# A fused two-block transformer kernel: relative bias skewed by DMA and spatial weights turned on VectorE, instead of on TensorE

## The reference, cut to what matters

```python
def diff_attention(q, k, v, lam, rel_bias):            # blocks of 128 queries
        bias = rel_bias[t5_bucket(kpos[None, :] - qpos[:, None])]   # (q, k, 4 heads)
        logits = jnp.where(mask, logits + bias[None, :, None], NEG_INF)
def gmlp_spatial_gate(u, vg, ln_g, ln_b, ws, bs):
    ws_m = jnp.where(mask[None], ws, jnp.zeros_like(ws))            # 8 groups of 128x128
    s = jnp.einsum('gij,bnjgc->bnigc', ws_m, vn) + ...
```

## Time and profile before

| what | value |
|---|---|
| median of 3 executions | 2445.34 us (2444.47 to 2445.42) |
| the profiled execution's own time | 2445.51 us |
| its span, first to last instruction | 2443.7 us |
| PE busy | 2425.7 us (99%) |
| DVE, ACT, POOL busy | 1378.2, 1161.1, 127.9 us |
| DMA queue of SP | 509.84 MB, 63.3% of 16 engines |
| mean granted TensorE clock | 0.998 |

### The profile page before, as it was taken

How to read it: one execution, slowest core, us unless ns; L and a number is a source line. 1 busy time by engine, 2 the same in 40 slices (tenths; PEclk the granted TensorE clock), 3 DMA queues, 4 the chain that set the end, 5 groups by cost and what they waited for, 6 DMA issues and landing times.

```text
span 2443.7 us, 28450 instructions
## 1 busy us (share of the span) xinstructions
PE 2425.7 (99%) x11416; PEld 2031.3 (83%) x11416; DVE 1378.2 (56%) x1113; ACT 1161.1 (48%) x1081; POOL 127.9 (5%) x144
## 2 busy tenths in 40 slices
PE   9999999999999999999999999999999999999998
PEld 7888888888888888888888889888888888888886
DVE  6877645656666666444555574554445444444445
ACT  5544554655556555333454364453343434433344
POOL 4000000001011110000000000000010100000000
PEclk9999999999999999999999999999999999999999
DMA  7566555587777777655565554556766767665553
GB/s 250 189 202 200 167 177 189 195 286 237 237 239 245 248 237 257 246 195 197 210 232 173 189 173 155 189 189 207 224 212 216 223 207 228 226 214 191 189 207 121
DMA packets 259456, 511.35 MB, mean 209 GB/s; under 512 B 10742, under 2 KB 33196, under 8 KB 258476
## 3 DMA queue, kind: packets, MB, share of 16 engines
q1 hardware_dynamic: 258936, 509.84, 63.3%
q10 hardware_dynamic: 436, 0.30, 0.0%
HBM read 482.83 MB, written 27.27 MB: 209 GB/s over the span
## 4 chain that ended last, share of the span: by engine, by line
PE 97%; ACT 1%; DVE 1%; issue 1%; DMA 0%; SPq 0%; DVEq 0%; ACTq 0%
PE ps L1256 28%; PE ps L1258 28%; PE ps L1257 28%; PE ps L1241 4%; PE ps L1242 2%; PE ps L1214 1%; PE ps L1250 1%; PE ps L1249 1%; PE ps L1248 1%; PE ps L1501 1%; ACT w_hi L683 1%; DMA raw<-in_w_in_dram 0%; DVE w_lo L1720 0%; PE ps L1516 0%; PE ps L1659 0%
## 5 line engine op out<-in xcount | busy, mean ns | idle before, releaser
L1720 DVE TENSOR_TENSOR w_lo<-raw,w_hi 128x2048 fp32r<-128x2048 f32 x427 | 988.1, 2314 | 1020.7 <-ACT w_hi L683 1020.4
L683 ACT ACTIVATE w_hi<-raw 128x2048 fp32r<-128x2048 f32 x427 | 818.5, 1917 | 1236.0 <-PE ps L1258 1113.7
L1256 PE MATMUL ps<-w_hi,xa 128*128 128x512 f32 x1856 | 724.8, 391 | 0.8 <-DVE w_lo L1720 0.8
L1258 PE MATMUL ps<-w_hi,xa 128*128 128x512 f32 x1856 | 723.0, 390 | 0.0
L1257 PE MATMUL ps<-w_lo,xa 128*128 128x512 f32 x1856 | 722.9, 390 | 0.0
L1256 PE MATMUL ps<-w_hi,g 128*128 128x512 f32 x1216 | 475.8, 391 | 0.0
L1258 PE MATMUL ps<-w_hi,g 128*128 128x512 f32 x1216 | 473.8, 390 | 0.0
L1257 PE MATMUL ps<-w_lo,g 128*128 128x512 f32 x1216 | 473.6, 390 | 0.0
L1256 PEld LDWEIGHTS ps<-w_hi,xa 128*128 128x128 f32 x1856 | 348.6, 188 | 73.9 <-issue 0.9
L1258 PEld LDWEIGHTS ps<-w_hi,xa 128*128 128x128 f32 x1856 | 348.5, 188 | 72.5
L1257 PEld LDWEIGHTS ps<-w_lo,xa 128*128 128x128 f32 x1856 | 348.6, 188 | 71.3
(11 more groups left out here) (316 smaller groups left out, 1367.8 us busy)
## 6 DMA issues: line engine op xcount, KB each, us to landing
raw<-in_ffn_w_dram SPq DMA_DIRECT2D x132, 1024.0 KB, 5.2
raw<-in_w_in_dram SPq DMA_DIRECT2D x95, 1024.0 KB, 5.2
raw<-in_w_up_dram SPq DMA_DIRECT2D x88, 1024.0 KB, 5.9
raw<-in_w_down_dram SPq DMA_DIRECT2D x44, 1024.0 KB, 5.1
raw<-in_w_out_dram SPq DMA_DIRECT2D x32, 1024.0 KB, 5.0
raw<-in_w_pg_dram SPq DMA_DIRECT2D x16, 1024.0 KB, 5.1
raw<-in_pl_w_gate_dram SPq DMA_DIRECT2D x16, 1024.0 KB, 5.1
up_turned_rows<-h SPq DMA_DIRECT2D x22, 512.0 KB, 3.0
```

What stands on the lines that cost most here:

```text
L683: A(w_hi[j % SPLIT][:, :], raw[s][:, :], ACT.Copy).then_inc(sem("w_hi_ready"), 1)
L1256: mm(o, high, hi, start=begin, stop=False)
L1258: return mm(o, low, hi, start=False, stop=end)
L1720: V.tensor_tensor(w_lo[j % SPLIT][:, :], raw[j % RAW][:, :], w_hi[j % SPLIT][:, :].bitcast(F32), ALU.subtract).then_inc(sem("w_lo_ready"), 1)
```

## The change

The bias row is now stored 128 times per head, in rows of pitch 384, and read back with a pitch of 383 from element 127: query row q then begins at 127 - q without a mirror. The store's source is the same four partitions, with a broadcast dimension. The spatial weights are turned by DVE in 32x32 blocks at position 4 of in2, stored by SP ahead of its load of chunk 10 of in2 and read back in four loads ahead of chunk 11. `flip`, `turn_masks`, `masks_read` and the two copies on ACT go. PE gets a wait for the turned weights in `spatial`; POOL masks the bias right after it has landed.

```diff
-        bias_dram = nc.dram_tensor("bias_rows", (4, 512), F32, kind="Internal").ap()
+        bias_dram = nc.dram_tensor("bias_rows", (4, P, S + P), F32, kind="Internal").ap()
...
-        ws_t = gw(11264, 1024).rearrange("p (n i) -> p n i", n=8)
+        ws_turned, ws_staged = gw(6144, 1024), gw(11264, 1024)
+        ws_t = ws_staged.rearrange("p (i n r) -> p n i r", i=4, r=32)
...
-        flip = xw(6656, P)
...
             def store_bias():
                 sp.wait_ge(sem("bias_row_ready"), 1)
-                sp.dma_start(bias_dram[:, 0:S + P - 1], bias_row[0:4, 0:S + P - 1]).then_inc(sem("bias_stored"), 16)
+                rows = bias_row[0:4, 0:S + P - 1].rearrange("p (o c) -> p o c", o=1).broadcast_to([4, P, S + P - 1])
+                sp.dma_start(bias_dram[:, :, 0:S + P - 1], rows).then_inc(sem("bias_stored"), 16)
...
-                skew = bass.AP(bias_dram.tensor, bias_dram.offset + hd * 512, [[1, P], [1, S]])
+                skew = bass.AP(bias_dram.tensor, bias_dram.offset + hd * P * (S + P) + P - 1, [[S + P - 1, P], [1, S]])
...
-            columns("in2", [(t["w_in_2"][0], 0), (t["w_in_2"][0], 512)], 1024, peel=5,
+            def put_ws(i):
+                if i == 1:
+                    sp.wait_ge(sem("ws_turned"), 1)
+                    sp.dma_start(up_turned_dram, ws_turned).then_inc(sem("ws_stored"), 16)
+            def take_ws(i):
+                if i == 1:
+                    sp.wait_ge(sem("ws_stored"), 16)
+                    for j in range(4):
+                        sp.dma_start(block_rows(ws_staged, j), block_column(up_turned_dram, j)).then_inc(sem("ws_back"), 16)
+            columns("in2", [(t["w_in_2"][0], 0), (t["w_in_2"][0], 512)], 1024, peel=5, at={2: put_ws, 3: take_ws},
...
-            pool.wait_ge(sem("h_ready"), H_READY["in2"] + 4)
-            then(pool.memset(flip, 0.0))
-            pool.affine_select(out=flip, in_=flip, compare_op=ALU.not_equal, fill=1.0,
-                               base=1 - P, pattern=[[1, P]], channel_multiplier=1).then_inc(sem("flip_ready"), 1)
...
-            pool.wait_ge(sem("bias_flipped"), 2)
+            pool.wait_ge(sem("bias_landed"), 64)
...
-            def masks_turned():
-                act.wait_ge(sem("ws_transposed"), 1)
-                A(gw(11264, 1024), bank(0, 2), ACT.Copy).then_inc(sem("ws_ready"), 1)
-                act.wait_ge(sem("bias_flipped"), 1)
-                A(gw(10240, 1024), bank(2, 2), ACT.Copy).then_inc(sem("bias_flipped"), 1)
...
-            def turn_masks():
-                pe.wait_ge(sem("banks_read"), G + 1)
-                pe.wait_ge(sem("ws_masked"), 1)
-                for n in range(8):
-                    last = nc.tensor.transpose(bank(0, 2)[:, n * P:(n + 1) * P], ws_in[:, n, :], ident[:, :])
-                last.then_inc(sem("ws_transposed"), 1)
-                pe.wait_ge(sem("flip_ready"), 1)
-                pe.wait_ge(sem("bias_landed"), 64)
-                for n in range(2):
-                    last = mm(bank(2 + n), flip, gw(10240 + 512 * n, 512), start=True, stop=True)
-                last.then_inc(sem("bias_flipped"), 1)
...
             def spatial():
                 pe.wait_ge(sem("vn_ready"), 1)
+                pe.wait_ge(sem("ws_back"), 64)
...
-                6: turn_masks,
-                8: masks_read,
...
+            def turn_ws():
+                dve.wait_ge(sem("ws_masked"), 1)
+                for a in range(2):
+                    last = V.transpose(block_columns(ws_turned, a), ws_in.rearrange("p n j -> p (n j)")[:, 512 * a:512 * (a + 1)]
+                                       .rearrange("p (k j c) -> p k j c", k=4, c=32))
+                last.then_inc(sem("ws_turned"), 1)
...
+                4: turn_ws,
```

More of the change, by code:

```diff
@@ L1136, in _ @@
                 1: lambda: token_roots("in2"),
-                6: masks_turned,
                 19: lambda: gate_gelu(0),
@@ L1618, in _ @@
             G = plan["in2"]["group"]
-            def turn_masks():
-                pe.wait_ge(sem("banks_read"), G + 1)
-                pe.wait_ge(sem("ws_masked"), 1)
-                for n in range(8):
-                    last = nc.tensor.transpose(bank(0, 2)[:, n * P:(n + 1) * P], ws_in[:, n, :], ident[:, :])
-                last.then_inc(sem("ws_transposed"), 1)
-                pe.wait_ge(sem("flip_ready"), 1)
-                pe.wait_ge(sem("bias_landed"), 64)
-                for n in range(2):
-                    last = mm(bank(2 + n), flip, gw(10240 + 512 * n, 512), start=True, stop=True)
-                last.then_inc(sem("bias_flipped"), 1)
-            def masks_read():
-                pe.wait_ge(sem("ws_ready"), 1)
-                pe.wait_ge(sem("bias_flipped"), 2)
             def late_maps():
```

## The result

The changed kernel takes **2456.87 us** (median of 5 executions, 2456.57 to 2457.62) against 2445.18 (5 executions): ratio 1.0047, interval [1.0036, 1.0058]. It is slower by 11.7 us. The profiled execution has a span of 2454.9 us against 2443.7.

The account below looks back on a forecast made before the run. PE was taken as the bound, busy 2425.7 of 2443.7 us. Stall 11.7 + clock 2.0 - removal 2.6 = +11.1 us gave 2456.5; the forecast's own range was 2451 to 2461, the 8-in-10 range 2442.5 to 2461.

Parts of the forecast that it names:

- The store's rate: Bias store in in1: partitions 0 to 3 yield 26.9 GB/s, so 784 KB take 29.2 us and land at 64.2 to 64.4.
- rival 1: Store in in1: four engines read at their own pace, landing before 52.6; only -2.6 us remain, 2442.8; chance 0.22.
- Four engines: Store in in1: its outermost 4 confines it to four engines, 25.4 GB/s each, lower bound 7.7 us.
- Who waits: End of lambda_sums in in1: DVE waits 14 to 15 us for the store, PE stalls before chunk 7, +11.7 us.
- The slope and the point of onset: PE's stall in in1: a store landing at T costs T - 52.6 us, one for one, nothing before 52.6.
- The second wait: Weight chunk 8 of in1 lands at 67.0 to 67.5, ready about 71.7; just covered by chunk 7, could cost up to 1 us.
- The clock: PE behind the 12 us stall in in1: some 4 us of work at half pace, +2.0 us (0 to 4).
- The removal: PE at chunk 6 of in2: eight transposes and four passes of the mirror product go, -2.6 us.
- the additions on DVE and SP in in2: Two block transposes on DVE (1.4 us), a 512 KB store, four loads and two waits on SP: cost 0.
- Rivals 2: Store in in1: a limit per partition, landing at 97, a stall of 44 us, 2489; chance 0.05.
- 3 (nothing given back in in2): In in2, DVE's transposes or the four loads make a low part 2 to 3 us late, store quick: 2445; chance 0.03.

Follow-up runs that it names:

- e4: Changed kernel with the four bias rows first moved to partitions 0, 8, 16 and 24, and the large store reading them there: 2442.98 us.
- e2: Changed kernel with 64 copies of each head's bias row instead of 128, read back in eight loads instead of four: 2442.39 us.
- e9: Changed kernel with 96 copies of each bias row instead of 128, queries 0 to 95 and 96 to 127 read apart: 2448.28 us.
- e3: Changed kernel with VectorE's wait for the bias store moved from position 4 to position 13 of in1: 2456.51 us.
- e5: Changed kernel with 44 extra products run on TensorE ahead of chunk 7 of in1, results unused: 2455.10 us.
- e1: Changed kernel with the bias back to small store, mirrored read and flip product; only the spatial weights turned on VectorE: 2445.72 us against 2445.48 before.
- e8: e2 with the spatial weights turned on TensorE as before, so only the flip product is gone: 2444.17 us against 2445.59 for the kernel before.
- e6: Changed kernel with a small store of one row per head, then copied 128 times from HBM to HBM; VectorE waits for the small store only: 2442.85 us.
- e7: e3 with the large store issued by ScalarE at position 2 of in1 instead of by SyncE, in its own queue: 2447.88 us.

## Why the prediction was right

It gave 2456.5 with the forecast's own range of 2451 to 2461; the time is 2456.87. By its steps:

- *The store's rate.* Forecast 26.9 GB/s, taken from loads of 32 partitions at a full share of busy engines; measured 784 KB from about 34.7 to 63.44, 27.3 GB/s on average: about 2 us of fast start, then a steady 25.5 GB/s, which the forecast did not tell apart. That a read shares the way as a write does was the open point (rival 1, 0.22). e4 settles it: other partitions, four times the rate. The port of 27.2 GB/s for partitions 0 to 3 that the Trainium skill gives ("SBUF — State Buffer", "Door 1: The DMA port swizzle") agrees with the average of 27.3; the steady rate of the trace is 6% below it. Four engines, read off the completion packets, fits a share of 0.22 to 0.26.
- *Who waits.* DVE for 14.3 us (14 to 15 forecast) and PE for 11.1 (11.7 forecast); most of the half microsecond is the landing, 63.44 instead of 64.3, since all of in1 began 0.4 us earlier in this execution and the average rate was a little higher. The slope and the point of onset hold in e2 (64 copies, no wait) and e9 (96 copies, 4.04 us).
- *The second wait* was forecast as just covered. It was covered by a wide margin: chunk 8 landed at 66.0 and its low part was ready at 70.3, while chunk 7 lasted till 74.0. e3 shows that it is real.
- *The clock.* 2.0 us forecast, 2.2 measured (e5 against the changed kernel). The term was worked out for a stall of 12 us, and the stall was 11. That it shrinks little with a shorter one I did not say: e9 lost 2.3 behind 4 us.
- *The removal.* -2.60 forecast, -2.60 measured in ACT's starts (the shift falls from 13.83 to 11.23 at chunk 6). Taken away singly, in e1 and e8, the transposes give 0.78 and the flip product 1.73, 0.1 less together. That the additions on DVE and SP in in2 cost nothing holds: DVE still had 1.86 us of idle time behind the transposes.
- *Not in the sum:* the pace of 5.65 us behind the stall, +0.6 us. It stands against the half microsecond of the stall, and so the total came out closer than its parts: that is luck, and not a finer forecast.

Rivals 2 (a limit per partition, 2489) and 3 (nothing given back in in2) are excluded by the rate and by the 5.55 us in in2. The versions without the slow store, e2, e4 and e6, are at 2442.4 to 2443.0, 14 us under the changed kernel and 0.10 to 0.12% under the kernel before, with intervals that end just below 1. The three cannot be told apart. e2 is the simplest.

## What to carry to other kernels

When work is moved from the bounding engine to DMA, price the transfer by where its bytes lie and not by their number alone: the broadcast out of partitions 0 to 3 ran at the rate of one engine though four worked on it, and in a shared queue it held up the weight chunks behind it. Read from the rows the moment at which somebody waits for it, the semaphore and the queue both; before that moment it cost nothing here, beyond it each microsecond counted once, and even a stall of 2.19 us (e7) brought the slow clock with it. If it is too slow, make fewer copies, spread the rows over the partitions, or copy inside HBM, before touching the wait.

## What was not expected

- The clock's price grows little with the stall. Behind idle times of 2.2, 4.0 and 11.1 us (e7, e9, the changed kernel) the chunk that followed lost 1.7, 2.3 and 2.4 us by PE's own starts, the slower pace included. Idle times of 0.38 us (e7) and 1.12 us (e5) left the granted clock at 1.00.
- TensorE's stream in this phase has two paces, 5.55 and 5.65 us a chunk, with no idle time in either. A pace holds for up to nine chunks and is worth up to 1 us. By the traces it ate the gain of e1 and not that of e2. In a kernel where 2 us are at stake, a change of 1 us on TensorE can therefore not be read off the time alone.
- The store began fast: 72 rows in the first 2 us and then 16 to 17 each microsecond. A short broadcast from the same partitions may therefore look quicker than a long one; no run tried it.
- Two queues on the same four engines share them: e7 let weight chunks pass a store that, in one queue, held them for 11 us.
